# Layer 1 window attention: the product with the values as three 64-column terms, added in the accumulator

## What is computed

```python
sc = jnp.einsum('bnqkgd,bnskd->bnkgqs', qb, kb).astype(jnp.float32) * scale + bias
sc = jnp.where(valid[None, :, None, None], sc, -jnp.inf)
m = jnp.maximum(jnp.max(sc, axis=-1, keepdims=True), sink_l)
p = jnp.exp(sc - m)
denom = jnp.sum(p, axis=-1, keepdims=True) + jnp.exp(sink_l - m)
o = jnp.einsum('bnkgqs,bnskd->bnqkgd', (p / denom).astype(v.dtype), vb)
...
return (oc * jax.nn.silu(gc)) @ w_out
```

## Time and profile before

| | |
|---|---|
| runs | 2847.64, 2850.52, 2851.12 us |
| the profiled execution | 2853.55 us, of which its span 2852.2 us |
| TensorE matmul busy | 2495.4 us (87% of the span) |
| weight load, VectorE, ScalarE, GpSimd busy | 2013.8, 1296.0, 1014.5, 654.5 us |
| chain that ended last | PE 67%, DVE 17%, ACT 8%, issue 6%, DMA 2%, POOL 1% |
| the window attention in the trace | first scores at 1252.63 us, last `MIX` begins at 1429.14 us |

### The profile page before, as it was taken

The page is one execution under the profiler, slowest core; times in us unless marked ns, Lnnn a source line. Parts: engine busy times, 40 slices in busy tenths (PEclk is TensorE's granted clock), DMA queues, the critical chain, the costliest instruction groups (busy, mean ns, idle before and its releaser), DMA issues.

```text
span 2852.2 us, 29535 instructions
## 1 busy us (share of the span) xinstructions
PE 2495.4 (87%) x11914; PEld 2013.8 (71%) x11914; DVE 1296.0 (45%) x1858; ACT 1014.5 (36%) x1508; POOL 654.5 (23%) x385
## 2 busy tenths in 40 slices
PE   3899788878887989989887999467989999999997
PEld 2687567757676868866675888246868888888885
DVE  6724399948997230049945100564232222222224
ACT  1321267757775121149833211531131111111111
POOL 0121122214552212245321222000222222222220
PEclk9999899999998999999998999665999999999998
DMA  6730000000002131100030111001111111111111
GB/s 245 244 113 25 11 1 1 1 15 1 1 1 88 39 104 46 51 11 1 1 111 23 52 52 30 12 0 30 59 52 48 49 45 45 45 45 45 52 45 59
DMA packets 158716, 135.25 MB, mean 47 GB/s; under 512 B 9686, under 2 KB 140020, under 8 KB 158068
## 3 DMA queue, kind: packets, MB, share of 16 engines
q1 hardware_dynamic: 158580, 133.35, 14.6%
HBM read 120.76 MB, written 12.58 MB: 47 GB/s over the span
## 4 chain that ended last, share of the span: by engine, by line
PE 67%; DVE 17%; ACT 8%; issue 6%; DMA 2%; POOL 1%; SPq 0%; DVEq 0%; ACTq 0%
PE ps L244 48%; PE ps L2117 9%; DVE NM L950 3%; DVE A_PTL L962 2%; DVE T L353 1%; DVE B_PTL L962 1%; DVE B_PR L954 1%; ACT C_PR L1444 1%; PE ps L921 1%; DVE HL L358 1%; PE ps L1933 1%; PE ps L911 1%; PE ps L934 1%; DVE A_PR L954 1%; DVE AC L445 1%
## 5 line engine op out<-in xcount | busy, mean ns | idle before, releaser
L244 PE MATMUL ps<-HH,WH 128*128 128x512 f32 (+1 forms) x2032 | 638.1, 395 | 60.7 <-DVE HL L358 28.7
L244 PE MATMUL ps<-HL,WH 128*128 128x512 f32 (+1 forms) x2032 | 632.3, 393 | 0.0
L244 PE MATMUL ps<-HH,WL 128*128 128x512 f32 (+1 forms) x2032 | 630.3, 392 | 0.0
L231 POOL TENSOR_TENSOR WL<-WR,WH 128x1024 fp32r<-128x1024 f32 (+2 forms) x137 | 317.6, 2318 | 1338.1 <-ACT WH L226 1337.9
L244 PEld LDWEIGHTS ps<-HH,WH 128*128 128x128 f32 (+1 forms) x2032 | 380.9, 189 | 151.7 <-issue 45.5
L244 PEld LDWEIGHTS ps<-HL,WH 128*128 128x128 f32 (+1 forms) x2032 | 384.7, 189 | 83.2
L244 PEld LDWEIGHTS ps<-HH,WL 128*128 128x128 f32 (+1 forms) x2032 | 383.6, 189 | 82.5
L2160 DVE TENSOR_TENSOR AT<-SG,ps 128x1024 f32<-128x1024 f32 x22 | 26.9, 1221 | 418.9 <-PE ps L244 418.9
L2132 ACT ACTIVATE SG<-ps 128x1024 f32<-128x1024 f32 x22 | 22.6, 1029 | 384.2 <-PE ps L244 384.2
L950 DVE TENSOR_REDUCE NM<-ps 128x1 f32<-128x1024 f32 x128 | 154.0, 1203 | 10.8 <-PE ps L911 10.7
L2165 DVE TENSOR_TENSOR X<-ps,X 128x1024 f32<-128x1024 f32 x88 | 107.8, 1225 | 112.0 <-PE ps L2117 111.9
(11 more groups left out here) (333 smaller groups left out, 4058.8 us busy)
## 6 DMA issues: line engine op xcount, KB each, us to landing
AW<-in_ada_w SPq DMA_DIRECT2D x12, 2048.0 KB, 8.4
WR<-in_w_ffn_in SPq DMA_DIRECT2D x44, 512.0 KB, 3.8
OW<-in_w_ffn_out SPq DMA_DIRECT2D x11, 1024.0 KB, 6.1
WR<-in_w_in SPq DMA_DIRECT2D x21, 512.0 KB, 3.8
WR<-in_odd_w_in SPq DMA_DIRECT2D x20, 512.0 KB, 3.8
WR<-in_even_w_in SPq DMA_DIRECT2D x17, 512.0 KB, 4.1
spill<-X SPq DMA_DIRECT2D x2, 4096.0 KB, 12.7
X<-spill SPq DMA_DIRECT2D x2, 4096.0 KB, 12.8
```

What stands on the lines that cost most here:

```text
L231: pool.tensor_tensor(WL[:, s, 0:w.kt, 0:w.m], WR[:, s, 0:w.kt, 0:w.m], WH[:, s, 0:w.kt, 0:w.m].bitcast(F32), ALU.subtract).then_inc(*w_low ...
L244: last = pe.matmul(ps[0:w.m, 2 * s + h, :], wt[:, s, k, 0:w.m], x[:, k, halves(h)], start=(k == 0 and n == 0), stop=(k == w.kt - 1 and n = ...
```

## The change

The product with the values takes only 64 columns of `C_VS` at a time, so its output has 64 rows, and there are three matmuls per key block, all added up in rows 0 to 63 of bank 6: high values by high probabilities, high values by low probabilities, low values by high probabilities. (The fourth term, low by low, which the stacked form also made, is no longer made.) `act_c_move`, `pool_c_mix` and the buffers `C_OT` and `C_O2` are gone. `dve_c_add` keeps its two instructions of 64 x 256, but each now multiplies the finished sum in `ps` by the gate `C_G` and writes to `MIX`. Everything that waited for `c_mixed` now waits for `c_added`.

```diff
@@ pe_c_values
-            for m, pt in enumerate((C_PTH, C_PTL)):
-                last = pe.matmul(ps[:, 6, :], C_VS[:, i % 2, lo + k, :], pt[:, g % 2, k, :, :].rearrange("p h n -> p (h n)"),
-                                 start=(k == 0 and m == 0), stop=(k == hi - lo - 1 and m == 1))
+            for m, (v, pt) in enumerate(((0, C_PTH), (0, C_PTL), (1, C_PTH))):
+                last = pe.matmul(ps[0:HD, 6, :], C_VS[:, i % 2, lo + k, rows(v, HD)],
+                                 pt[:, g % 2, k, :, :].rearrange("p h n -> p (h n)"),
+                                 start=(k == 0 and m == 0), stop=(k == hi - lo - 1 and m == 2))
@@ dve_c_gate
-            dve.wait_ge(*c_mixed.at(g - 2))
+            dve.wait_ge(*c_added.at(g - 2))
@@ dve_c_add
-        dve.wait_ge(*c_moved.at(g))
-        if g >= 2:
-            dve.wait_ge(*c_mixed.at(g - 2))
+        i, n = g // TT, g % TT
+        dve.wait_ge(*c_summed.at(g))
+        dve.wait_ge(*c_gated.at(g))
         for e in range(2):
-            high, low = (x.rearrange("p (t e n) -> p e t n", t=2, e=2)[:, e]
-                         for x in (ps[0:HD, 6, :], C_OT[0:HD, :]))
-            last = dve.tensor_tensor(C_O2[g % 2][rows(e, HD), :].rearrange("p (t n) -> p t n", t=2), high, low, ALU.add)
+            last = dve.tensor_tensor(MIX[rows(e, HD), 2 * i:2 * i + 2, rows(n)],
+                                     ps[0:HD, 6, :].rearrange("p (t e n) -> p e t n", t=2, e=2)[:, e],
+                                     C_G[rows(e, HD), g % 2, :].rearrange("p (t n) -> p t n", t=2), ALU.mult)
         last.then_inc(*c_added.up(g))
@@ act_c_move and its call
-    def act_c_move(g):
-        act.wait_ge(*c_summed.at(g))
-        act.activation(C_OT[0:HD, :], ps[HD:P, 6, :], ACT.Copy).then_inc(*c_moved.up(g))
@@ pool_c_mix and its call
-        pool.tensor_tensor(mix, C_O2[g % 2][:, :].rearrange("p (t n) -> p t n", t=2),
-                           C_G[:, g % 2, :].rearrange("p (t n) -> p t n", t=2), ALU.mult).then_inc(*c_mixed.up(g))
@@ sp_odd_out, act_odd_out, dve_odd_out
-        sp.wait_ge(*c_mixed.at(NG - 1))
+        sp.wait_ge(*c_added.at(NG - 1))
```

More of the change, by code:

```diff
@@ L1244, in build @@
     C_SB, C_PR = place("C_SB", 51, [P, 4, WIN + 1]), place("C_PR", 133.5, [P, 4, WIN + 1])
-    C_OT, C_O2 = place("C_OT", 139.53125, [P, HALF]), [place("C_O20", 141.53125, [P, 2 * P]), place("C_O21", 117.75, [P, 2 * P])]
     AWAY, C_RID, C_G = place("AWAY", 75, [P, WIN]), place("C_RID", 76.5, [P, 2 * P]), place("C_G", 77.5, [P, 2, 2 * P])
@@ L1471, in act_attention_c @@
                 act_c_high(u - 1)
-            if u % 2 == 0 and 4 <= u < NU + 4:
-                act_c_move((u - 4) // 2)
             i = u // 16 + 1
@@ L1537, in pool_attention_c @@
                 pool_c_wide((u - 2) // 2)
-            if u % 2 == 1 and 5 <= u < NU + 5:
-                pool_c_mix((u - 5) // 2)
             i = u // 16 + 1
@@ L1575, in act_odd_out @@
     def act_odd_out():
-        act.wait_ge(*c_mixed.at(NG - 1))
+        act.wait_ge(*c_added.at(NG - 1))
         act_high(ODD_OUT[0])
@@ L1592, in dve_odd_out @@
     def dve_odd_out():
-        dve.wait_ge(*c_mixed.at(NG - 1))
+        dve.wait_ge(*c_added.at(NG - 1))
         dve_no_squares(2)
```

## The result

| | before | changed |
|---|---|---|
| median of the runs | 2850.52 us (2847.64 to 2851.25, 5 runs) | 2864.16 us (2862.99 to 2867.09, 5 runs) |
| ratio | | 1.0050, 95% interval 1.0035 to 1.0065 |
| profiled execution, its span | 2853.55, 2852.2 us | 2864.16, 2862.7 us |
| first value matmul to the read of `X` | 1265.24 to 1429.89, 164.65 us | 1263.19 to 1438.23, 175.04 us |
| first `OUT` to the end | 2834.85 to 2852.2, 17.4 us | 2843.39 to 2862.7, 19.3 us |

The kernel became slower by 13.6 us, where 13.9 was forecast. The last two rows of the table say at once that this agreement is better than the working deserves: the attention grew by 10.4 us only, and 1.9 us more lie at the very end of the program, where nothing was changed. No trace places the remaining 1.3 us.

What follows compares the result with a forecast made beforehand. Bound: a closed attention loop of value matmuls, scores, VectorE's bias and add, 5.34 us per full block. Terms 20.5 - 3.6 - 1.0 - 0.6 - 1.4 = +13.9 us, median 2850.5 to 2864.4 us, range 2858 to 2871.

Steps and rivals of the forecast that it cites:

- the loop: Attention block of 5.34 us: value matmuls to scores 1.57, to bias 0.83, to add's end 2.79, to next values 0.15.
- hidden: Rival: TensorE's idle time in the attention takes in the new matmuls, +1.2 us in sum, 2851.7 us; chance 0.07.
- faster: Rival: ScalarE's exponential behind the move is late in every block, so removing the move gives 2838.5 us; chance 0.03.
- the trace's own test on group 16: Group 16's block, two value matmuls fewer, took 4.87 us, 0.47 less; taken as showing value matmuls are not hidden.
- The third matmul: 88 value matmuls added on TensorE in the attention at 0.233 us each, +20.5 us; 0.70 per full block.
- the 6 with one `C_QH`: Blocks with one extra ScalarE copy: without the move they grow 0.54 in place of 0.70 us, six times, -1.0 us.
- Blocks after a group with n = 7: Short blocks with two key blocks, charged two added value matmuls, +0.47 us each, like all short ones.
- one for one: Rule that an attention block's length follows its number of value matmuls, at 0.235 us each.
- ScalarE's relief: Without the move, three `C_KH` blocks go from 6.81 to 6.32 us, 1.19 back each against the 0.70 charged: -3.6 us.
- The end of the attention: Last groups without ScalarE's move: -0.6 us at group 30, -1.4 us from group 31 to the read of `X`.
- Nothing behind the attention is touched: Claim that after the attention `odd_out` only starts 13.9 us later and takes as long.
- drain: Rival: new change of form between transposes and values costs up to 0.09 us x 32, 2.9 us, 2867.3; chance 0.11.

Runs made afterwards that it cites:

- r2: Changed kernel with two 64-column matmuls per key block, the product of the low part of the values left out; 2843.11 us against 2849.09, ratio 0.9976.
- r3: Kernel before with a third stacked 128-column matmul per key block, move, add and mix kept; 2870.67 us against 2849.09, ratio 1.0067.
- r4: Changed kernel with a 64 x 512 copy put back on ScalarE where the move stood, groups 0 to 29; 2868.04 us against 2849.09, ratio 1.0064.
- r10: Changed kernel with 20 one-column matmuls (80 instructions) added in TensorE's idle start; 2862.01 us against 2849.64, ratio 1.0041.
- r7: Changed kernel with each group's product split, four of nine matmuls moved behind the next odd unit's scores; 2847.87 us against 2850.19, ratio 0.9991.
- r9: Kernel before with 44 one-column matmuls (176 instructions) added in TensorE's idle start; 2855.79 us against 2849.64, ratio 1.0022.
- r1: The changed kernel run again without an edit, beside the kernel before; 2864.17 us against 2849.09, ratio 1.0046.
- r5: Changed kernel with 40 one-column matmuls added in TensorE's idle start; 2864.37 us against 2850.19, ratio 1.0049.
- r6: Kernel before with 88 one-column matmuls (352 instructions, 176 meant) added in TensorE's idle start; 2851.57 us against 2850.19, ratio 1.0005.
- r8: Changed kernel with the product split in two and 40 one-column matmuls added at the start; 2846.34 us against 2850.19, ratio 0.9989.

## Why the prediction was right, and where its working was not

The direction, the place and the loop were right. Of the loop's four steps three came out as forecast, and the first is 2.19 us where 2.27 was. The two rivals that would have hidden the cost are refuted: *hidden* by r2 and r3, each of which moves the number of matmuls alone, and *faster* by r2 and r4. But 13.9 against 13.6 us is luck: the attention was forecast 3.5 us too long, and time outside it made that up. One piece of the evidence was luck too, the trace's own test on group 16, where two matmuls fewer seemed to give 0.47 us:

```profile
1348.45 0.83 DVE L1393 TENSOR_TENSOR C_O<-ps,C_OT 64x256 f32<-64x256 f32 x2
...
1349.08 0.88 PE L1307 MATMUL ps<-IDENT,C_PR 128*128 128x128 f32 x6 [0.31 <-ACT C_PR L1444]
...
1349.40 0.59 DVE L1355 CUSTOM_DVE_ANT_0 C_SB<-ps,BF,NSINK 128x384 f32<-128x384 f32 x1
...
1353.60 0.83 DVE L1393 TENSOR_TENSOR C_O<-ps,C_OT 64x256 f32<-64x256 f32 x2
...
1354.56 0.59 DVE L1355 CUSTOM_DVE_ANT_0 C_SB<-ps,BF,NSINK 128x384 f32<-128x384 f32 x1
```

VectorE has no pause in this block, 5.16 us from bias to bias (1349.40 to 1354.56), so VectorE set its length and not the value matmuls. It read as 4.87 because the first value matmul, at 1349.71, was late: it stood behind transposes that waited for ScalarE's exponential, and began 0.43 us after the adds had ended, where the loop has 0.15. In r2, with four matmuls in such a block too, the start is not late, and the block takes VectorE's 5.15 us (key heads 1 to 3) beside 5.26 in a plain full block: 0.11 less, not 0.47. That a matmul in the loop costs 0.23 us is shown by r2 and r3, not by this pair. The four terms against what the blocks show, all as differences to the kernel before:

- **The third matmul, +20.5 us.** Within a stream the distance was 0.230 us, as taken. But the first distance of a product fell from 0.30 to 0.32 us to 0.25 or 0.26, so a plain full block grew by 0.61 to 0.65 and not by 0.70. Over the 14 plain blocks (-0.9) and the 6 with one `C_QH` (+0.45, forecast 0.54: -0.5) that is 1.4 us less. I had priced only the distance in a stream; the 32-column rows show nothing of the first one behind another form. r3 has the price of the same 88 matmuls at full width, a plain block of 6.01, or +0.68.
- **Blocks after a group with n = 7, charged +0.47 each like all short ones.** They grew by 0.09. In the kernel before they took 4.90 us, where the loop with four value matmuls and the narrow low part adds up to about 4.6. Another path was already longer, ScalarE's: the first two of the rows above are the end of such a block, with the transposes, and the values behind them, waiting for the exponential that stood behind the move. r2, which has no move, takes 4.62 us with the same four matmuls. So the added time found cover in ScalarE's relief, which the prediction had put at nothing here: 1.1 us in three blocks. r3 says the same with +0.12 to +0.15. The rule "one for one" was read off the other kind of short block, where it was luck, and not checked on this one.
- **ScalarE's relief, -3.6 us in three `C_KH` blocks.** The step that failed is "ScalarE's move took 0.49 us of that, so this block becomes 6.32". It became 5.95, the loop. In the kernel before, `C_KH` began 0.14 us after the block did; changed, it begins 0.24 us before:

```profile
1358.00 2.14 ACT L1424 ACTIVATE C_KH<-KC 64x1024 fp32r<-64x1024 f32 x2
...
1361.53 0.87 PE L1306 MATMUL ps<-IDENT,C_PR 128*128 128x128 f32 x6 [0.30 <-ACT C_PR L1444]
...
1363.27 0.79 ACT L1452 ACTIVATE C_PTH<-ps 128x768 fp32r<-128x768 f32 x1
...
1364.19 0.42 PE L1327 MATMUL ps<-C_PTH,C_VS 128*64 128x512 f32 x1
```

  6.81 - 0.49 - (0.14 + 0.24) = 5.94. This meets the loop's 5.95, but the loop is what holds the block (VectorE's bias waits 0.71 us for the scores there). ScalarE's own time shows in r2: 6.04 to 6.07 us from the start of `C_KH` to the next value product, where the kernel before has 6.67, and a start 0.24 to 0.36 us ahead of the block, so ScalarE alone would let these blocks be 5.68 to 5.82. An engine with room reaches its heavy stretch earlier relative to the others, and that lead counts beside the removed instruction. r4, with the copy put back, has 0.65 to 0.80 more in these blocks. The three blocks shrank by 2.3 us where a shrinking by 1.5 was forecast.
- **The end of the attention, -2.0 us with group 30.** Measured: group 30 took 3.28, as before, and group 31's end 2.50 in place of 3.49. With the three and two matmuls that they gained this is 0.2 us better than forecast.

The attention so came to +10.4 us in place of +13.9 (short by 1.4, 1.1, 0.8 and 0.2 in these four points). What filled most of the gap in the measured medians is the end of the program, +2.0 and +2.3 in the two profiles, which the prediction had declared untouched ("Nothing behind the attention is touched"). The instructions there were not; the packet of code among them has moved. In r10, with the packet moved out, the end is 17.4 us again. Attention and end together give 12.3 to 12.7 us, the medians 13.6 and 15.1. The remainder is not only scatter: in all eleven comparisons here the medians differ by more than these two stretches do, by 0.2 (r7) to 4.7 us (r9, whose attention is the old one). Where it lies is open; outside attention and end the profiled executions differ by up to 6 us from each other, too much to read it off.

The rival *drain* had 0.09 us per block for the new change of form between transposes and values. In the full blocks there is no trace of it: the transposes begin 0.75 us before the values (1381.30 and 1382.05) in the changed kernel, and 0.76 before (1376.97 and 1377.73). There the values wait for the multiply, which could hide it. The traces of r7 separate the two: where its first part stands behind six transposes and the multiply has been over for 0.2 us or more, the values begin 0.63 us after the transposes, and in the kernel before 0.63 us too where they did not wait for the adds. So the new change of form costs nothing that can be read, and the rival fails.

## What to carry to other kernels

When three engines are all near 90% busy, look for the loop that closes in the timeline, write its steps down with their times, and count an added instruction by whether it stands in that loop. A block of the same kernel that has fewer such instructions is a ready experiment, but check it on every kind of block, and that no other engine works through it without a pause. And a loop that is closed by the order on one queue can be opened by the order: moving four of nine matmuls behind the scores gave back 15 us of attention, more than the whole change had cost, without removing any work. The same split in the kernel before was not run, so whether three 64-column terms are worth having once the order is changed stays open.

## What was not expected of the hardware

A packet of TensorE's code, 0.02 MB, lands about every 29 us, and where it falls among back-to-back 512 KB writes of the output, one `OUT` waits 2.85 (r9) to 3.98 us (r4) for its buffer in place of 1.48. Of the twelve profiles, the six with a packet in the last 15 us (the changed kernel, r1, r3, r4, r7, r9) take 18.8 to 19.9 us from the first `OUT` to the end, and the six without one (the kernel before, r2, r5, r6, r8, r10) take 17.4. Adding 176 instructions ahead moves the packet there (r3, r9, the change itself), 256 move it out again (r10), to 32 or 33 us before the end as in the kernel before. The count fits TensorE's code: before, 23828 matmuls and weight loads come with 95 packets, 251 to each. So a change in the number of instructions can cost some 2 us hundreds of microseconds behind it. In all six with the packet, and in none of the others, one pair of writes has the slow tail shown above. From 2852.2 to 2854.7 us it is some 40 KB in single packets, about the share of one of the 16 DMA engines in a 512 KB write (32 KB, an estimate), so it looks as if the packet held up one engine. That the packet is the cause, and not something that goes with it, is still inferred: the trace does not name the engine that carried it.

The width of the loaded operand counted at most once per product and not per matmul: 0.230 us apart at 64 as at 128 columns, with weight loads of 0.134 and 0.188 us. Between the first two there are 0.25 or 0.26 us at 64 columns where the product had waited for the multiply, and 0.30 to 0.32 where it stood right behind the transposes (the four groups with n = 0 of the changed kernel, and most products of r7); at 128 columns there are 0.30 to 0.32 either way.
